# Seven-product down projections for three of four chunks, with GpSimdE adding their results into x

## What is computed

```
x = x + 0.5 * swiglu(rms_norm(x, g_ffn1), w1_ffn1, w3_ffn1, w2_ffn1)
...mixer: sliding-window attention and chunked gating, projections w_in and w_out
x = x + 0.5 * swiglu(rms_norm(x, g_ffn2), w1_ffn2, w3_ffn2, w2_ffn2)

def swiglu(x, w1, w3, w2):
    return (jax.nn.silu(x @ w1) * (x @ w3)) @ w2
```

## Time and profile before

| | |
|---|---|
| runs of the kernel | median 968.97 us of 3 (968.1 to 968.98) |
| the profiled execution | span 965.8 us (first to last instruction; the page gives no other time for it), 19305 instructions |
| TensorE / VectorE / ScalarE / GpSimdE busy | 99% / 70% / 47% / 23% |
| granted TensorE clock, mean | 0.998 of full speed (2.4 GHz) |
| DMA | 100.33 MB, 104 GB/s over the span |
| first feed-forward stage, from its first unit to its last down product | about 60 to 371 us |
| second feed-forward stage, the same | about 585 to 896 us |

### The profile page before, as it was taken

The page is one execution under the profiler, slowest core; times in us unless marked ns, Lnnn a source line. Parts: engine busy times, 40 slices in busy tenths (PEclk is TensorE's granted clock), DMA queues, the critical chain, the costliest instruction groups (busy, mean ns, idle before and its releaser), DMA issues.

```text
span 965.8 us, 19305 instructions
## 1 busy us (share of the span) xinstructions
PE 953.1 (99%) x7942; PEld 941.7 (98%) x7942; DVE 676.0 (70%) x1078; ACT 456.9 (47%) x750; POOL 225.3 (23%) x136
## 2 busy tenths in 40 slices
PE   7999999999999999999999999999999999999997
PEld 7999999999999999899999999999999999999997
DVE  6999568757678563557974499767766768855576
ACT  7645325533534444565545465434443443534243
POOL 0211111311111226300218412112311101114621
PEclk9999999999999999999999999999999999999999
DMA  8931524153143327312133783243324315235302
GB/s 242 176 95 48 164 70 117 53 156 89 44 134 108 99 77 210 80 45 67 45 87 101 137 170 110 82 116 98 99 85 127 94 57 143 67 99 163 89 23 89
DMA packets 190098, 100.33 MB, mean 104 GB/s; under 512 B 12986, under 2 KB 187412, under 8 KB 189996
## 3 DMA queue, kind: packets, MB, share of 16 engines
q1 hardware_dynamic: 176612, 90.27, 33.0%
q0 software_dynamic: 9360, 4.72, 3.9%
q10 hardware_dynamic: 4040, 4.12, 1.4%
HBM read 96.54 MB, written 3.59 MB: 104 GB/s over the span
## 4 chain that ended last, share of the span: by engine, by line
PE 90%; DVE 5%; ACT 2%; issue 1%; DMA 1%; SPq 0%; ACTq 0%; DVEq 0%
PE ps L1801 48%; PE ps L1879 37%; PE ps L2233 2%; PE ps L1835 2%; DMA x_rows<-in_x_prompt_dram 1%; DVE w_lo L1499 1%; PE ps L2135 0%; PE ps L2106 0%; DVE tt L1517 0%; DVE tt L1510 0%; DVE probs L1542 0%; ACT w_hi L744 0%; ACT tt L957 0%; PE ps L2257 0%; DVE ab L1394 0%
## 5 line engine op out<-in xcount | busy, mean ns | idle before, releaser
L1879 PE MATMUL ps<-xo_lo,w_hi 128*128 128x260 f32 x1008 | 284.7, 282 | 0.0
L1879 PE MATMUL ps<-xo_hi,w_lo 128*128 128x260 f32 x1008 | 284.4, 282 | 0.0
L1879 PE MATMUL ps<-xo_hi,w_hi 128*128 128x260 f32 x1008 | 284.1, 282 | 0.0
L1801 PE MATMUL ps<-h_hi,w_hi 128*128 128x260 f32 x960 | 194.6, 284 | 0.7 <-DVE x L1410 0.7
L1801 PE MATMUL ps<-h_hi,w_lo 128*128 128x260 f32 x960 | 193.0, 283 | 0.0
L1801 PE MATMUL ps<-h_lo,w_hi 128*128 128x260 f32 x960 | 192.9, 282 | 0.0
L1879 PEld LDWEIGHTS ps<-xo_hi,w_lo 128*128 128x128 f32 x1008 | 189.8, 188 | 0.0
L1879 PEld LDWEIGHTS ps<-xo_lo,w_hi 128*128 128x128 f32 x1008 | 189.7, 188 | 0.0
L1879 PEld LDWEIGHTS ps<-xo_hi,w_hi 128*128 128x128 f32 x1008 | 189.6, 188 | 0.0
L1801 PEld LDWEIGHTS ps<-h_hi,w_hi 128*128 128x128 f32 x960 | 147.5, 188 | 1.2 <-issue 1.0
L1801 PEld LDWEIGHTS ps<-h_lo,w_hi 128*128 128x128 f32 x960 | 148.2, 188 | 0.0
(11 more groups left out here) (286 smaller groups left out, 1447.4 us busy)
## 6 DMA issues: line engine op xcount, KB each, us to landing
w_raw<-in_w_ffn_dram SPq DMA_DIRECT2D x88, 256.0 KB, 3.0
w_a<-in_w_ffn_dram SPq DMA_DIRECT2D x36, 512.0 KB, 4.7
w_raw<-in_w_ffn_dram SPq DMA_DIRECT2D x48, 384.0 KB, 3.2
w_raw<-in_w_ffn_dram SPq DMA_DIRECT2D x16, 512.0 KB, 6.0
w_raw<-in_w_in_dram SPq DMA_DIRECT2D x10, 512.0 KB, 4.0
w_lo<-in_w_ffn_dram POOLq DMA_DIRECT2D x9, 512.0 KB, 7.6
w_raw<-in_w_ple_gate_dram SPq DMA_DIRECT2D x8, 512.0 KB, 3.6
x_rows<-in_x_prompt_dram SPq DMA_DIRECT2D x8, 256.0 KB, 6.3
```

Of the source, the lines that this page charges most:

```text
L1801: ins = pe.matmul(ps[:, bank + step * h, 0:HALF], w[:, c, w0:w0 + P], m_[:, sk, h * HALF:(h + 1) * HALF], start=(first and n == 0), stop=( ...
L1879: ins = pe.matmul(ps[:, b, 0:Q], w[:, c, k * P:(k + 1) * P], m_[:, op, k, :], start=(first and k == 0 and n == 0), stop=(k == 3 and n == 2 ...
```

## The change

Three of the four down chunks (pairs 0-2, 3-5 and 6-7) become units too: 4 units of two output tiles each, where the two halves of k are the even and the odd tiles of each pair, so a product has 3, 3 or 2 k tiles (9, 9 or 6 matmuls). A stage now has 30 units, numbered 0 to 29: up units of pairs 2 and 3 are 0 to 3, the first down group is 4 to 7, up pairs 4, 5, 6 are 8 to 13, the second group 14 to 17, up pairs 7 and 8 are 18 to 21, the third group (2 k tiles) 22 to 25, up pairs 9 and 10 are 26 to 29. The last chunk stays as it was. With it come:

- seven operands of h per pair for pairs 0 to 7 (`hop_hi`, `hop_lo`): four sums of the blocks, made by three VectorE instructions (`h_sum`), rounded by ScalarE (`hs_hi`), low halves by GpSimdE (`hs_lo`, 1040 elements); the three plain blocks by `h_hi` and `h_lo` (780 elements);
- `w_lo_24` moves from VectorE to GpSimdE in every unit;
- the result of a down unit is combined into `ab` or `bb`, and GpSimdE adds it into x (`dn_add`, 1040 elements) in place of VectorE's `x_add` from PSUM; the factor 0.25 moves into the gate;
- a down unit's weights are loaded in four transfers and go through the steps of a unit (sums, high and low halves);
- `snap` moves in SBUF, and the a22 and a21 parts are loaded by two transfers in place of one.

```diff
+LAGGED = (3, 6, 8)
+UNITS = tuple(u for p in range(2, KF // 2) for u in (
+    [("up", p, 0), ("up", p, 1)] + [("dn", LAGGED.index(p), m) for m in range(KD // 2) if p in LAGGED]))
-H_LO_BY_DVE = (0, 1, 7, 10)
+H_LO_BY_DVE = (0, 1, 10)
...
+    for p in range(2, KF // 2 - 1):
+        n = UNIT_OF[("up", p, 1)]
+        put(n + 1, "d", ("gate", p))
+        put(n + 2, "a", ("h", p))
+        if p in LAGGED:
+            n = UNIT_OF[("up", p + 1, 0)]
+        else:
+            n += 2
+            if p < KF // 2 - 2:
+                put(n, "b", ("h_hi", p))
+                put(n, "c", ("h_sum", p), ("h_lo", p))
+                put(n, "d", ("hs_hi", p), ("hs_lo", p))
...
+        if p < N_STRASSEN:
+            put(n, "c", ("h_hi", p), ("h_sum", p))
+            put(n, "d", ("h_lo", p), ("hs_hi", p))
+            put(n, "e", ("hs_lo", p))
...
+        if n:
+            steps.append(("c21", n - 1))
+            if UNITS[n - 1][0] == "dn":
+                steps.append(("dn_add", n - 1))
```

On GpSimdE:

```diff
+                    elif kind == "w_lo_24":
+                        j, = arg
+                        g = N_UNIT * s + j
+                        pool.wait_ge(unit_hi, 4 * g + 3)
+                        nc.gpsimd.tensor_tensor(w_cells(wl, s, j, "s2", 2), w_cells(w_raw, s, j, "s2", 2),
+                                                w_cells(wh, s, j, "s2", 2).bitcast(F32),
+                                                ALU.subtract).then_inc(unit_lo24, 1)
...
+                    elif kind == "hs_lo":
+                        p, = arg
+                        pool.wait_ge(hs_hi_ready, N_STRASSEN * s + p + 1)
+                        nc.gpsimd.tensor_tensor(flat(hop_lo[:, H_SLOT[p], 3:7, :]), flat(hop_raw[:, H_SLOT[p], 3:7, :]),
+                                                flat(hop_hi[:, H_SLOT[p], 3:7, :]).bitcast(F32),
+                                                ALU.subtract).then_inc(hs_lo_ready, 1)
+                    elif kind == "dn_add":
+                        n, = arg
+                        g = N_UNIT * s + n
+                        m = 2 * UNITS[n][2]
+                        pool.wait_ge(combined, 3 * g + 3)
+                        pool.wait_ge(c21_done, g + 1)
+                        if UNITS[n][1]:
+                            pool.wait_ge(x_added, N_ADDED * s + 4 * UNITS[n][1])
+                        nc.gpsimd.tensor_tensor(flat(x[:, m:m + 2, :]), flat(result(n)), flat(x[:, m:m + 2, :]),
+                                                ALU.add).then_inc(x_added, 1)
```

On VectorE and TensorE:

```diff
+                    elif kind == "h_sum":
...
+                        nc.vector.tensor_tensor(raw_h[:, U1:T3 + 1, :], ab[:, 1:4:2, :],
+                                                ab[:, 0:1, :].broadcast_to([P, 2, Q]),
+                                                ALU.subtract).then_inc(h_summed, 1)
...
+                kn = k_tiles(n)
...
+                for k in range(kn):
+                    if kind == "up":
+                        hi, lo = xo_hi[:, op, k, :], xo_lo[:, op, k, :]
+                    else:
+                        p = CHUNKS[c][k]
+                        hi, lo = hop_hi[:, H_SLOT[p], op, :], hop_lo[:, H_SLOT[p], op, :]
```

More of the change, by code:

```diff
@@ L92, in ffn_loads @@
     loads = [("up", (0, 1, 2)), ("up", (3, 4, 5)), ("up", (6, 7))]
[L93 to L99, removed]
+    loads += [("unit", n) for n in range(N_UNIT)]
+    return loads + [("down", ms) for ms in LAST_GROUPS]
 def ffn_steps():
@@ L110, in prep @@
             return [("w", "next", r) for r in range(3)]
-        kind, *arg = loads[i]
+        kind, arg = loads[i]
         if kind == "unit":
[L113 to L116, removed]
+            return [(name, arg) for name in UNIT_STEPS]
+        return [("w", kind, n) for n in arg]
     side = {
@@ new lines, in ffn_steps, with put @@
+    for n in range(N_STD):
+        steps.append(("up", n))
+        steps += side[n]
+    at = {}
+    def put(n, place, *what):
+        at[(n, place)] = at.get((n, place), []) + list(what)
+    put(0, "a", ("h_hi", 0), ("xo_lo", 6))
+    put(0, "b", ("h_sum", 0))
+    put(0, "d", ("h_lo", 0), ("hs_hi", 0), ("hs_lo", 0))
+    put(1, "c", ("swi_b", 3))
+    put(1, "d", ("h_hi", 1))
+    put(2, "a", ("h_sum", 1), ("h_lo", 1))
+    put(2, "c", ("hs_hi", 1), ("hs_lo", 1))
+    for p in range(2, KF // 2 - 1):
[10 more added lines that the diff above has]
+                put(n, "d", ("hs_hi", p), ("hs_lo", p))
+            else:
+                put(n, "c", ("h_hi", p))
+                put(n, "d", ("h_lo", p))
+            continue
+        if p < N_STRASSEN:
+            put(n, "c", ("h_hi", p), ("h_sum", p))
+            put(n, "d", ("h_lo", p), ("hs_hi", p))
+            put(n, "e", ("hs_lo", p))
+        else:
+            put(n, "a", ("h_hi", p))
+            put(n, "c", ("h_lo", p))
@@ L224, in weight_plan @@
             elif kind == "down_b":
-                key = ("down", s, 3, arg[0])
+                key = ("down", s, arg[0])
             if key:
@@ L363, in hybrid_decoder_layer @@
         sq = sb("sq", [P, T])
+        with ExitStack() as under:
+            snap = sb("snap", [P, 3, Q], scope=under)
         ssq = sb("ssq", [P, T])
@@ L601, in lo_wait, with slot_read @@
                 eng.wait_ge(lo_in[i % 2], 16 * (i // 2 + 1))
+        def slot_read(s, p, r):
+            c = max(c for c in range(3) if CHUNKS[c][-1] < p and any(H_SLOT[i] == H_SLOT[p] for i in CHUNKS[c]))
+            return done[("prod", s, UNIT_OF[("dn", c, KD // 2 - 1)], r)]
         def std_key(s, arg):
```

476 lines of the change are left out of this document (254 added, 222 removed).

## The result

The changed kernel takes 1087.14 us (median of 4 runs, 1083.08 to 1087.4), the kernel before 968.54 in the same comparison: a ratio of 1.1218, 95% interval 1.1199 to 1.1237. It is slower, as forecast, but by 118.6 us where 73 were predicted, and 2 us beyond the range.

What follows compares the result with a forecast made beforehand. TensorE bounds the kernel, busy 953.1 of 965.8 us. 965.8 less 23.0 for 192 saved matmuls, plus 48 us of waits a stage (ends 20 and 70), plus 3.2 from span to median, gives 1042.0 us; range 983 to 1085.

Steps and rivals of the forecast that it cites:

- The ledger's waits: Feed-forward stages: VectorE's and GpSimdE's summed SBUF claims, 297.8 us a stage against TensorE's 260.0, leave 48 us of waits.
- GpSimdE's price: What a GpSimdE instruction takes from VectorE on their shared SBUF path: 1.10 us for 512 elements, 2.20 for 1024.
- the rival of whole durations: GpSimdE's instructions cost VectorE their full length, 14 us more per stage, so 1070 (1065 to 1085); chance 0.12.
- The rival of starved short units: Third group's 2-k-tile units: preparations, adds and loads follow each other, each late link adding time; above 1085; chance 0.07.
- a floor of 10.1: Units 21-26: least TensorE wait from SBUF claims of 52.5 us against TensorE's 40.2, with a lag of 2.2 off.
- The forecast's 48: Waits per stage: 44 us at best, up to 12 more for uncovered evictions, 3 to 4 less for late low halves.
- 965.8 - 23.0 + 2x48 + 3.2: Whole kernel: span, less saved matmuls, plus two stages' waits, plus span-to-median difference; 1042.0 us.
- SyncE ... for the same bytes ... so nothing.: Weight loads: 240 issued against 156 for the same bytes, DMA share 0.25 to 0.45; costed at nothing.
- ScalarE "at nothing": ScalarE's added evictions and 16 roundings lie beside the products; at most a late last copy, 1 us a stage.
- The forecast that the waits stand on low halves and evictions: Product matmuls' waits on VectorE's and GpSimdE's low halves and evictions head the list, most in units 2-8 and 11-18.
- VectorE's mean for 1024 elements: Sign in the changed profile: VectorE's 1024-element low half rises well above 1291 ns though it has fewer of them.
- wrong if units 2 to 8 take less than 85 us: Refutation sign: the prediction is wrong if this stretch of a feed-forward stage takes less than 85 us.

Runs made afterwards that it cites:

- e8_memset: Changed kernel with GpSimdE's feed-forward low halves replaced by memsets that read nothing, and its additions into x cut to 64 columns: 957.55 us.
- e2: Changed kernel with the low halves of s2 and s4 moved from GpSimdE back to VectorE: 1059.2 us.
- e3: Changed kernel with the 24 additions into x moved from GpSimdE to VectorE: 1070.8 us.
- e11: Changed kernel with only a22's low half made by a negated ScalarE copy and an adding DMA instead of GpSimdE's subtraction: 1057.5 us.
- e10: Changed kernel with GpSimdE's feed-forward arithmetic moved to VectorE, a22's low half by ScalarE copy and adding DMA, slot tables turned, hidden-sum rounding later: 962.9 us.
- e5: Changed kernel with ScalarE's rounding of the hidden sums moved behind the copy of product 6: 1082.7 us.
- e12: Changed kernel, GpSimdE's feed-forward arithmetic on VectorE, a22's low half by ScalarE copy and adding DMA, slot tables turned, early hidden-sum rounding kept: 961.6 us.

## Why the prediction was wrong

**Right.** That the kernel gets slower by waits of TensorE; TensorE's bound and the price of a matmul: without waits the sum was to be 942.8 us of span, and e8_memset has 955.8, the 13 us between them being boundary and product waits (6.6 and 2.8), their restart and the clock at those places. The ledger's waits: 2 x 48 = 96 us forecast, 93.4 measured, in the stretches named. GpSimdE's price below whole durations: the rival of whole durations, whose 1070 (1065 to 1085) came nearer than 1042, wanted 124 us of waits, and there were 93.4. The rival of starved short units named the time that came, above 1085, but not its cause: the third group's stretch has 10.8 us of waits against a floor of 10.1, and no wait at a product ends on a DMA. That these numbers were nearer is an accident of the terms that were missing.

**How far the ledger carries.** Its level came out within 3 us, its differences did not. Taking 26 (e2), 13 (e3) and 27 us (e11) a stage out of it lowered the waits by 12, 7 and 9 us a stage, where some 20, 9 and 13 to 22 were expected; e10 left 6.6 a stage where 0 to 3 were. The forecast's 48 itself was picked between 44 and 56 by a guess at how many evictions have GpSimdE beside them. So that 96 met 93.4 is in part luck, and no run measures GpSimdE's price by itself.

**The step that failed.** The sum took a wait at its length: "965.8 - 23.0 + 2x48 + 3.2". Every matmul behind it was priced at 0.1197 us. 58 us of them ran at the lower clock, which lost some 29 us, and each wait has 0.16 us of restart, 8 us. The forecast's span was 1038.8 and the measured one is 1085.6: of these 46.8 us the clock is 29, the restart 8, the stage boundaries 7.2 (next paragraph), the waits 2.6 fewer than forecast, and 5 stay unassigned. Without the clock's 29 the time would have been 1058, inside the range. The profile of before could not show this, as TensorE never stood there for long between units; the missing bound was a second end for the price of a matmul, twice the first, on some part of the forecast's 96 us of waits.

**The term that was costed at nothing.** "SyncE ... for the same bytes ... so nothing." The bytes cost nothing, but the number of loads turned from odd to even, and with it the half of the slots in which the stage ends: 7.2 us of waits and 3 of clock. The text looked at the DMA share and at the short units, not at what follows the stage.

**ScalarE "at nothing".** It allowed 1 us a stage for the last copy of a unit; e5 took 7 us of waits away, 3.4 a stage, and e12 shows none of it once the port is free. So it nearly held in the sum, but the list of waits names ScalarE for 73.5 of 93.4 us. The forecast that the waits stand on low halves and evictions was wrong as to where they are seen.

**The signs.** VectorE's mean for 1024 elements rose from 1291 to 1725 ns, as said (1633 with the smaller sizes among them). GpSimdE's 1040-element low half did not rise (2571 against 2572 ns): its addition into x, of the same size, did (3207 from `ab`, 2919 from `bb`), and the low half of s2 and s4 (2821 for 1024 elements, against 2.41 us at 516.36). The bound "wrong if units 2 to 8 take less than 85 us" was badly set: they took 80.7, and TensorE needs 60.3 for them without a wait, so even with the ledger's whole floor of 19.5 us for units 0-8 they come to 79.8. By its own sign the prediction was wrong where its ledger was not.

**The range.** It ended at 1085, from the waits alone. With the 0.3 us of clock per us of wait that was measured (29 over 93.4), its upper end of 2 x 70 us of waits would have come to about 1130, an estimate.

## What to carry to other kernels

Before work is moved to an idle GpSimdE, add up what both it and VectorE want with SBUF inputs, per stretch, and compare that sum with TensorE's time there: the sum is the bound, not either engine's share. Take it for the sign and the place of the waits; the size that it gives for a single move was up to twice too large here. Work that must leave VectorE is better given to an engine or a queue outside this pair (here a negated copy on ScalarE and an adding DMA). Price a forecast wait of TensorE of 2.5 us and more above its length, for the clock behind it; and when the number of loads changes, follow the slots past the end of the stage.
